# Odd mixer of a two-block transformer kernel: tokens stored column by column, 512 keys per attention unit, later key/value products and two output tiles woven between the steps

## What is computed

```python
def odd_mixer(z, zc, ...):
    xp, q, k, v = jnp.split(z @ w_in, ODD_SPLIT, axis=-1)      # 512 wide each, 8 heads of 64
    q, k = rms_norm(q per head, q_gain), rms_norm(k per head, k_gain)
    kc, vc = jnp.split(zc @ w_in[:, C_W + D_W:], 2, axis=-1)   # 256 context keys and values
    y = concat([multiscale_pool(xp, w_pool, c_scale),
                neighbourhood_attn(q, k, v, kc, vc, rpb)]) @ w_out

def neighbourhood_attn(...):      # GRID_W = 64, rows = 8, NA_ROWS = 8, NA_COLS = 16
    qcol = np.arange(GRID_W).reshape(nqb, NA_COLS)
    qstart = np.clip(qcol - NA_COLS // 2, 0, GRID_W - NA_COLS)
    ...
    col_valid = (kcol >= qstart) & (kcol < qstart + NA_COLS)
    s_loc = q . k * scale + rpb[row distance, column distance];  s_loc = where(col_valid, s_loc, NEG)
    p = softmax(concat([s_loc, s_ctx]));   o = p . [v, v_ctx]
```

## Time and profile before

| | us |
|---|---|
| median of 3 runs | 3572.13 |
| lowest, highest | 3567.84, 3575.3 |
| span of the profiled execution | 3565.0 |
| odd mixer: products `OX` and `OKV` | 2070 to 2191 |
| odd mixer: between the last `OKV` product and the first unit | 2191 to 2232 |
| odd mixer: 32 attention units | 2232 to 2360 |
| odd mixer: `OO` | 2360 to 2403 |

### The profile page before, as it was taken

One profiled execution on the slowest core, in us unless ns is written; L12 is line 12 of the kernel. 1 busy time (PEld: TensorE's weight loads), 2 busy tenths in 40 slices (PEclk: granted clock), 3 DMA queues, 4 the chain that ended last, 5 costly groups with the idle time before them and its releaser, 6 DMA issues.

```text
span 3565.0 us, 45562 instructions
## 1 busy us (share of the span) xinstructions
PE 3463.3 (97%) x19212; PEld 3191.4 (90%) x19212; DVE 1998.8 (56%) x3139; ACT 974.1 (27%) x1446; POOL 40.8 (1%) x97
## 2 busy tenths in 40 slices
PE   8999999999999999999999999899999999999998
PEld 6999999898999999999999998677888878877777
DVE  6757655578466664465553454854334755455654
ACT  4211113266311111221111221543222322332232
POOL 0000000000000000000000000000000000000000
PEclk9999999999999999999999998999999999999999
DMA  5343422100234331234332131112222310211122
GB/s 212 125 129 118 137 83 76 48 30 7 69 116 129 124 124 58 65 97 130 120 127 74 60 105 40 30 54 86 98 95 95 120 42 13 78 60 62 50 92 80
DMA packets 85338, 308.32 MB, mean 86 GB/s; under 512 B 9680, under 2 KB 9872, under 8 KB 83344
## 3 DMA queue, kind: packets, MB, share of 16 engines
q1 hardware_dynamic: 81216, 290.04, 24.9%
q0 software_dynamic: 3920, 15.37, 1.3%
HBM read 301.18 MB, written 4.19 MB: 86 GB/s over the span
## 4 chain that ended last, share of the span: by engine, by line
PE 87%; DVE 8%; issue 2%; ACT 2%; DMA 1%; SPq 0%; POOL 0%; DVEq 0%; ACTq 0%
PE psum L414 77%; DVE nmx L1340 1%; PE psum L1758 1%; PE psum L1093 1%; PE psum L1780 1%; PE psum L1288 1%; PE psum L1279 1%; DMA adaw<-in_ada_w 1%; DVE od_s L1337 1%; DVE wl L407 1%; PE psum L2233 1%; PE psum L1106 1%; PE psum L2242 1%; PE psum L2681 0%; PE psum L1271 0%
## 5 line engine op out<-in xcount | busy, mean ns | idle before, releaser
L414 PE MATMUL psum<-zh,wh 128*128 128x384 f32 (+2 forms) x3792 | 1139.0, 359 | 23.3 <-DVE zhf L2539 4.6
L414 PE MATMUL psum<-zh,wl 128*128 128x384 f32 (+2 forms) x3792 | 1112.5, 352 | 0.0
L414 PE MATMUL psum<-zl,wh 128*128 128x384 f32 (+2 forms) x3792 | 1111.8, 352 | 0.0
L414 PEld LDWEIGHTS psum<-zh,wh 128*128 128x128 f32 x3792 | 697.3, 190 | 79.2 <-issue 28.2
L414 PEld LDWEIGHTS psum<-zh,wl 128*128 128x128 f32 x3792 | 697.9, 190 | 43.3
L414 PEld LDWEIGHTS psum<-zl,wh 128*128 128x128 f32 x3792 | 698.4, 190 | 42.4 <-issue 4.3
L407 DVE TENSOR_TENSOR wl<-raw,wh 128x1024 fp32r<-128x1024 f32 (+2 forms) x415 | 489.9, 1181 | 314.4 <-ACT wh L397 313.7
L397 ACT ACTIVATE wh<-raw 128x1024 fp32r<-128x1024 f32 (+2 forms) x415 | 419.9, 1020 | 863.7 <-PE psum L414 649.4
L758 DVE TENSOR_TENSOR scr<-psum,rf 128x768 f32<-128x768 f32 x132 | 126.4, 958 | 399.5 <-PE psum L414 399.5
L414 PE MATMUL psum<-hidh,wh 128*128 128x384 f32 (+1 forms) x1232 | 336.6, 342 | 0.0
L414 PE MATMUL psum<-hidl,wh 128*128 128x384 f32 (+1 forms) x1232 | 336.5, 342 | 0.0
(11 more groups left out here) (403 smaller groups left out, 2789.3 us busy)
## 6 DMA issues: line engine op xcount, KB each, us to landing
raw<-in_wup SPq DMA_DIRECT2D x176, 512.0 KB, 3.4
raw<-in_mod_w SPq DMA_DIRECT2D x128, 512.0 KB, 3.3
raw<-in_wdn SPq DMA_DIRECT2D x64, 448.0 KB, 3.4
raw<-in_w_sw SPq DMA_DIRECT2D x36, 512.0 KB, 3.2
raw<-in_wdn SPq DMA_DIRECT2D x32, 512.0 KB, 4.2
adaw<-in_ada_w SPq DMA_DIRECT2D x8, 1024.0 KB, 15.6
raw<-in_od_in SPq DMA_DIRECT2D x16, 512.0 KB, 3.2
raw<-in_w_ga SPq DMA_DIRECT2D x16, 512.0 KB, 3.3
```

The lines of the kernel that those rows point to most:

```text
L414: last = nc.tensor.matmul(psum[:, at + to:at + to + e - s], w[:, wslot(n), q * P:(q + 1) * P], x[:, q, s:e], start=(q == 0 and j == 0), st ...
```

## The change

Own tokens of queries, keys and values are now stored column by column (token = column x 8 + row): the drain (`drain_columns`) writes with a stride of 8 elements and rotates the queries by 8 columns. A unit is now 16 columns by 8 rows of queries, and the keys that these may see lie in 32 columns, that is 256 own keys; with 256 context keys a unit has 512. Three of the four units of a head take two neighbouring blocks of 128 own keys, the fourth (columns 56 to 63 and 0 to 7) takes the first and the last block. `nbias` is 768 columns. Transposes and value products go from 6 to 4 blocks.

The stage `OKV` is split: `OKV0` holds the first head pair's key and value tile and runs as before; the other six tiles (three head pairs), now in the order key, value, key, value and all in slot 0, are woven in: 6 chunks before the first unit and 42 in steps 0 to 23. Sums, roots, spreads and value transposes of a head pair sit between steps too, pool and query sums behind `OX` and `OKV0` tiles. ScalarE alone copies the attention output, back into `ox`; later `odd_cat_hi`/`odd_cat_lo` make the rounded parts and restore the row order. The first two `OO` tiles run chunk by chunk: chunks 0 to 6 in steps 27 to 33, chunk 7 last. The stage `OO` uses accumulators of 512 columns. The helpers `heads_*`, `att_*` and `Group` lose what only the odd mixer used. Outside the odd mixer the instructions of every queue stand as before.

The diff, cut to its core:

```diff
-            stages += [Stage("od_in_x", 8, KD, "x+"), Stage("od_in_kv", 8, KD, "full+"),
-                       Stage("od_out", 8, KD, "x")]
+            stages += [Stage("od_in_x", 8, KD, "x+"), Stage("od_in_kv0", 2, KD, "full+"),
+                       Stage("od_in_kv", 6, KD, "full+"), Stage("od_out", 8, KD, "x")]
+            stages[-2].alone = True
+            stages[-1].pitch = 512
...
+        class OddUnit:
...
+                if self.n < 3:
+                    at, self.bias = self.n * P, nbias[:, self.hd % 2, 0:512]
+                    self.keys = [(k[:, at:at + 256], 0, 256), (k[:, TX:T], 256, 256)]
+                    tiles = (self.n, self.n + 1, 4, 5)
+                else:
+                    self.bias = nbias[:, self.hd % 2, 256:768]
+                    self.keys = [(k[:, TX:T], 0, 256), (k[:, 0:P], 256, P), (k[:, 3 * P:TX], 256 + P, P)]
+                    tiles = (4, 5, 0, 3)
...
+            def scores(self):
+                return psum[:, O_S + self.i % 2 * 512:O_S + self.i % 2 * 512 + 512]
+
+            def probs(self):
+                return od_s[:, self.i % 3, :]
...
+        OD_BEFORE = (2, 1, 1, 1, 1)
+        OD_CHUNKS = [2, 2, 2, 2, 2, 2, 1, 1] * 3
...
+        OD_END = [next(i for i in range(24) if sum(OD_BEFORE) + sum(OD_CHUNKS[:i + 1]) >= KD * (k + 1))
+                  for k in range(OKV.tiles)]
...
+        OD_DRAIN = {e + 1: k for k, e in enumerate(OD_END)}
+        K_SUM, K_FACTOR, K_SPREAD, K_LATER = [{e + a: k // 2 + 1 for k, e in enumerate(OD_END) if k % 2 == 0}
+                                              for a in (2, 3, 4, 5)]
+        K_SQUARE = {e + 1: k // 2 + 1 for k, e in enumerate(OD_END) if k % 2 == 0}
+        V_TURN, V_LATER = [{e + a: k // 2 + 1 for k, e in enumerate(OD_END) if k % 2} for a in (2, 3)]
+        OD_CAT = {25: (0, 1), 26: (2, 3), 27: (4,), 28: (5,), 29: (6,)}
+        OD_OUT = {27: 0, 28: 1, 29: 2, 30: 3, 31: 4, 32: 5, 33: 6}
...
+        def out_chunk(pe, q):
+            pe.wait_ge(o_cat_lo, q + 1)
+            for n in OO.n[0:2]:
+                if q == 0:
+                    weights_ready(pe, n)
+                last = chunk_products(OO, n, q, zh, zl)
+                if q == KD - 1:
+                    last.then_inc(tile_done, 1)
...
+        def odd_cat_hi(act, c):
+            if c == 0:
+                act.wait_ge(tile_done, done(OKV.n[-1]))
+            if c < 4:
+                act.wait_ge(pool_cp, c + 1)
+            else:
+                act.wait_ge(at_o, OU0 + 8 * (c - 4) + 8)
+            x, like = cat_source(c)
+            nc.scalar.activation(like(zh[:, c, TC:T]), x, ACT.Copy).then_inc(o_cat_hi, 1)
...
         def odd_pe(pe):
-            products(pe, OX, zh, zl, **beside_first(pe, 4))
-            products(pe, OKV, zh, zl)
-            pe.wait_ge(drained, all_drained(OKV))
-            for a in range(6):
-                if a >= 2:
-                    pe.wait_ge(ovt_cp, a - 1)
-                for m in range(4):
-                    last = nc.tensor.transpose(psum[:, 3072 + a % 2 * 512 + m * P:3072 + a % 2 * 512 + (m + 1) * P],
-                                               okv[:, 4 + m, a * P:(a + 1) * P], ident[:])
-                last.then_inc(ovt_tr, 1)
-            pe.wait_ge(od_loaded, 32)
-            for g in range(4):
-                pe.wait_ge(pool_in, g + 1)
-                nc.tensor.matmul(psum[:, g * 512:g * 512 + TX], wpool[:, g, :], ox[:, g, :],
-                                 start=True, stop=True).then_inc(pool_mm, 1)
-            pe.wait_ge(pool_lo, 4)
-            heads_pe(pe, "odd")
-            after_heads(pe, "odd")
-            pe.wait_ge(ovt_cp, 6)
-            att_pe(pe, "odd")
-            pe.wait_ge(at_o, NU_ODD)
-            products(pe, OO, zh, zl)
...
+            def border(k):
+                if k >= 6:
+                    pool_sum(pe, k - 6)
+                    q_sum(pe, k - 6)
+            products(pe, OX, zh, zl, **beside_first(pe, 4), then=border)
+
+            def later(k):
+                if k == 0:
+                    pool_sum(pe, 2)
+                    pool_sum(pe, 3)
+                q_sum(pe, 2 + k)
+            products(pe, OKV0, zh, zl, then=later)
+            run = Along(OKV)
+            for turn, count in enumerate(OD_BEFORE):
+                if turn == 1:
+                    k_sum(pe, 0)
+                if turn in (2, 3):
+                    odd_spread(pe, 0, turn - 2)
+                if turn == 4:
+                    v_turn(pe, 0, 0)
+                chunks_pe(pe, run, count)
+            v_turn(pe, 0, 1)
+            pe.wait_ge(pool_cp, 4)
+            pe.wait_ge(drained, all_drained(OKV0))
...
+            for i in range(NO + 3):
+                if i < NO:
+                    score(i)
+                if 2 <= i < NO + 2:
+                    transposes(i - 2)
+                if i >= 3:
+                    values(i - 3)
+                if i in K_SUM:
+                    k_sum(pe, K_SUM[i])
+                if i in K_SPREAD:
+                    odd_spread(pe, K_SPREAD[i], 0)
+                if i in K_LATER:
+                    odd_spread(pe, K_LATER[i], 1)
+                if i in V_TURN:
+                    v_turn(pe, V_TURN[i], 0)
+                if i in V_LATER:
+                    v_turn(pe, V_LATER[i], 1)
+                along_pe(pe, run, od_chunks(i))
+                if i in OD_OUT:
+                    if OD_OUT[i] == 0:
+                        pe.wait_ge(drained, all_drained(OKV))
+                    out_chunk(pe, OD_OUT[i])
+            out_chunk(pe, KD - 1)
+            products(pe, OO, zh, zl, first=2)
...
+                if 2 <= i < NO + 2:
+                    u = OUNITS[i - 2]
+                    act.wait_ge(at_t, u.u + 1)
+                    if i >= 4:
+                        act.wait_ge(at_pv, u.u - 1)
+                    nc.scalar.activation(od_pt[:, i % 2, :], psum[:, O_PT:O_PT + 512], ACT.Copy).then_inc(at_pc, 1)
+                if i < NO:
+                    u = OUNITS[i]
+                    act.wait_ge(at_s, u.u + 1)
+                    nc.scalar.activation(u.probs(), u.probs(), ACT.Exp, bias=nmx[:, u.k:u.k + 1],
+                                         accum_out=rsum[:, u.k:u.k + 1]).then_inc(at_e, 1)
+                if i >= 3:
+                    u = OUNITS[i - 3]
+                    act.wait_ge(at_pv, u.u + 1)
+                    for c, to, w in u.out:
+                        ins = nc.scalar.activation(ox[u.r, 4 + u.m, to:to + w], u.sums()[u.r, c:c + w], ACT.Copy)
+                    ins.then_inc(at_o, 1)
+                if i in K_SQUARE:
+                    k_square(act, K_SQUARE[i])
+                if i in K_SUM:
+                    od_root(act, K_SUM[i] + 1)
+                if i in K_FACTOR:
+                    k_repeat(act, K_FACTOR[i])
+                if i in V_TURN:
+                    v_copy(act, V_TURN[i], 0)
+                if i in V_LATER:
+                    v_copy(act, V_LATER[i], 1)
+                beside_splits(act, run, od_chunks(i), split_hi)
+                for c in OD_CAT.get(i, ()):
+                    odd_cat_hi(act, c)
...
+                    for first, end in ((turned, GW), (0, turned))[:1 + (turned > 0)]:
+                        at = (first - turned) % GW
+                        ins = nc.vector.tensor_tensor(to[:, :, at:at + end - first], x[:, :, first:end],
+                                                      f[:, :, first:end], ALU.mult)
...
+            def scale_scores(u):
+                m = nmx[:, u.k:u.k + 1]
+                dve.wait_ge(at_qk, u.u + 1)
+                if u.i > 2:
+                    dve.wait_ge(at_t, u.u - 2)
...
+                if i in OD_DRAIN:
+                    drain_kv(OD_DRAIN[i])
+                if i in K_FACTOR:
+                    od_reciprocal(dve, K_FACTOR[i] + 1)
+                if i < NO:
+                    scale_scores(OUNITS[i])
+                beside_splits(dve, run, od_chunks(i), split_lo)
+                if 1 <= i <= NO:
+                    divide(OUNITS[i - 1])
+                if i in K_SPREAD:
+                    odd_k_norm(dve, K_SPREAD[i], 0)
+                if i in K_LATER:
+                    odd_k_norm(dve, K_LATER[i], 1)
+                for c in OD_CAT.get(i - 1, ()):
+                    odd_cat_lo(dve, c)
+            odd_cat_lo(dve, KD - 1)
```

621 lines of the change are left out of this document (356 added, 265 removed).

## The result

| | before | after |
|---|---|---|
| median of 4 runs, us | 3572.12 | 3531.17 |
| lowest, highest | 3567.84, 3575.3 | 3527.15, 3533.83 |
| profiled execution: its span | 3565.0 | 3532.0 |

The change makes the kernel faster: ratio 0.9886, 95% interval 0.9872 to 0.9900, 41.0 us by the medians. The forecast was 65.9 us and 3506, with a range up to 3524. So the direction held, and 25 us of the expected gain are missing.

The account below looks back on a forecast made before the run. TensorE, 97% busy near full clock, was taken as the bound. A 169.0 us stretch was to become 70.7 + 20.2 + 12.2, saving 65.9 us: forecast 3506 us, range 3492 to 3524.

Parts of the forecast that it names:

- term 1 (the unit): Attention units on TensorE: 2.21 us each with 512 keys against 3.29 before; 32 units take 70.7 us.
- Term 2 (the work ahead of attention): Value transposes, pool products, sums and spreads, kept in full but moved between products: 20.2 us at full clock.
- Term 3 (the waits): TensorE waits that stay or are new in the woven stretch, from first woven chunk to third output tile: 12.2 us.
- tile ends: Five later steps where a woven key/value tile completes and is drained: TensorE waits 4.3 us in sum.
- A clock that falls inside the loop: Listed sign of being wrong; expected instead no stretch with TensorE over 90% busy and a clock below 1.
- The step from span to median: 65.9 us saved gives a span of 3499.1; the median, lying 7.1 us above the span, gives 3506.2.
- Table switches: Rival: six ScalarE table loads of 1.28 us in the loop delay exponentials by 7.7 us: 3514; chance 0.08.
- Strided writes: Rival: drains' strided writes cost twice the strided row, 14 us plus 2 us at the last rounding: 3522; chance 0.06.
- A period of 4.0 us per unit: Rival: the unit's chain keeps its mean period despite 512 keys, losing 13 us: 3519; chance 0.06.
- Lock-step: Rival, slower: attention runs one unit at a time, 7.2 us each, 22 us more than before: 3594; chance 0.04.
- a change that does not do what it says: Rival: the woven chunks are not in the attention loop; no size or separate chance given.
- The check by other stages: Two already woven stages idle TensorE 4.4% and 6.8%, implying 6 to 9 us in the loop against 9.9 listed.

Follow-up runs that it names:

- division first: Changed kernel with one VectorE edit: the division of the unit before comes ahead of the next weight tile's low part; 3508.56 us, ratio 0.9825.
- high part first: Changed kernel with one ScalarE edit: the weight tile's high part comes ahead of the step's exponential instead of at its end; 3506.7 us, ratio 0.9821.
- both: Changed kernel with ScalarE's high part ahead of the exponential and VectorE's low part last in the step; 3504.07 us, ratio 0.9810.

## Why the prediction was right and wrong

**What bounds the kernel, and term 1 (the unit), held.** After, a step at full clock has scores at 2245.29, transposes at 2246.15, values at 2246.59 and the next work at 2247.48: 0.86, 0.44 and 0.89 us, against 0.87, 0.44 and 0.90.

**Term 2 (the work ahead of attention) held in size.** At full clock twelve key sums take 1.26 us (0.105 each, 0.11 counted) in the kernel with the division first. In the change some of them ran at half clock, 2.42 us for twelve. One price was missing: the first pair of product matmuls behind other work takes 0.43 to 0.44 us from start to start where the following pairs take 0.35, and for 512 columns 0.31 against 0.23. That happens some 36 times, about 3 us by this estimate, which the prediction put at nothing.

**Term 3 (the waits) failed in one item.** The first woven chunk waited 1.52 us (1.5 counted), step 1 1.44 (1.53), the end 2.68 + 0.25 (3.4), the first key pair nothing (0.8). But the division waits are 14.8 us, of which five are tile ends with 12.2 where 4.3 were counted, and step 2 has 2.64 where 0.6 was. The failing step is the sentence "drain 2.15, scores 1.5, split 1.2 and then division 0.55 make 5.6 us". Its four numbers add up to 5.4, and the 0.2 more is not explained; that is small. It adds up VectorE's own instructions and takes the low part as a cost of 1.2 us without asking what it waits for. The prediction's order fences showed the low part ahead of the division, and ScalarE's high part was in the diff, behind the exponential, the output copy and the squares. With the order changed on either engine, the time is within 2.4 us of the forecast.

**The clock was the second failing step.** That no busy stretch would have a clock below 1 was stated as what would show, not derived. It was 0.50 for 37.5 us, and costs 11.3 us by the medians with the waits filled, 16.4 by the mixer. "A clock that falls inside the loop" stood among the signs of being wrong, and came. The trace of before had shown 0.67 in a stretch with gaps; that the same could follow gaps of 2 to 3 us in a loop that is 90% busy was not priced. Added up for the mixer: 9 us more of waits (21.2 in all where 12.2 were counted), 16.4 of clock and 3 of returns to the products make 28 of the missing 29.3.

**The step from span to median.** Taking 65.9 us off the median was sound, but 7.1 us is no fixed distance. A run's time is its span plus 1.7 to 1.9 us in every execution here (3533.83 and 3532.0). The other 5.3 of the 7.1 us belong to before's profiled execution alone, which was quicker than any timed run. For this reason the two profiled spans differ by only 33.0 us, and because the profiled execution of after has 10 us of half clock around 700 and 890 us, in unchanged stages, where that of before has none.

**The rivals.** Table switches: no, 3529.65 without them, and no drain of 1.38 us is seen, so the Trainium skill's rule ("ScalarE: Activation LUTs", section "Rules for kernel authors"), to batch one table set, has no price at this place. The load is 1.28 us here too. Strided writes: a drain of 512 columns takes 1.09 us, near the 1.02 of the strided row, not its double; but 4 to 8 us hung on it, which the sum had only in part. A period of 4.0 us per unit: no, 2.38. Lock-step, and a change that does not do what it says: no.

**The check by other stages misled.** Idle shares of 4.4% and 6.8% seemed to confirm 9.9 us; the loop has 17.0 of 167, 10%. Those stages have an order of their own, and their shares say nothing of this one.

## What to carry to other kernels

Before work is woven into a loop, write down for each in-order queue what each instruction waits for, and not only how long it takes: an instruction off the critical path that waits for another engine, ahead of one on the path, makes its wait everybody's. Price a gap of TensorE at more than its length where the clock follows it (here, taking away 12.7 of 14.8 us of waits gave 24.5). And run each half of a change by itself: here the shorter units alone, even with one accumulator for the tiles in front, gave all of its gain.

## What the hardware showed

- Single waits of TensorE of 2 to 3 us, in a loop that is 90% busy, were followed by 3.4 to 10.2 us at a granted clock of 0.50; two profiled executions of the changed kernel show it at the same places. Not every such wait is: the one of 2.68 us at the end of the loop was followed by none in both, and by 3.4 us of half clock in three kernels with another order (division first, high part first, both). With the waits filled by matmuls whose result nobody reads, the clock stayed at 1.00 and the kernel was 11 us faster, its mixer 16.4 us. The Trainium skill, "TensorE: Matmul & The Clock Gate", section "HAM oscillation — how this bites in real kernels", prices such time as one half of it. By that, an estimate, 37.5 us would cost 18.8; the run with filling shows 11.3 by the medians and 16.4 by the traces, and the measurement decides.
- A VectorE write with a stride of 8 elements took 1.09 us for 128x512, a little more than the strided read's 1.02, against 0.69 for contiguous ones.
- Of the spread between executions of one kernel, up to 13 us, a part is half clock in stages that are the same in all: 10.2 us around 700 and 890 in one execution of the changed kernel, 3.4 in another. What starts it there, no run tells.
